# Memory attention in a hybrid encoder layer: its value products as three rounded passes over split operands, one fill place later

## Reference, cut to what matters

```python
proj = x @ w_in                       # r_q, r_k, ..., a_q, a_z are columns of it
mk, mv = jnp.split(mem @ xa_w_kv, 2, axis=-1)
s = jnp.einsum('blhd,bmhd->bhlm', q, mk).astype(jnp.float32) * XA_DH ** -0.5
p = jax.nn.softmax(s, -1)
xa = jnp.einsum('bhlm,bmhd->blhd', p, mv.astype(jnp.float32))
xa = xa * jax.nn.silu(a_z)
```

## Time and profile before

| | |
|---|---|
| Median of 3 runs | 1772.15 us (1770.97 to 1772.45) |
| The profiled execution | 1769.98 us, of which its span is 1767.8 us |
| PE busy | 1728.8 us, 98% of the span |
| PEld, DVE, ACT, POOL busy | 1438.5 (81%), 1034.6 (59%), 594.2 (34%), 538.2 (30%) us |
| Chain that ended last, by engine | PE 85%, DVE 7%, DMA 3%, ACT 2% |
| Granted TensorE clock | 0.998 of full speed over the span |

### The profile page before, as it was taken

The page is one execution under the profiler, slowest core; times in us unless marked ns, Lnnn a source line. Parts: engine busy times, 40 slices in busy tenths (PEclk is TensorE's granted clock), DMA queues, the critical chain, the costliest instruction groups (busy, mean ns, idle before and its releaser), DMA issues.

```text
span 1767.8 us, 22844 instructions
## 1 busy us (share of the span) xinstructions
PE 1728.8 (98%) x8848; PEld 1438.5 (81%) x8848; DVE 1034.6 (59%) x2022; ACT 594.2 (34%) x829; POOL 538.2 (30%) x342
## 2 busy tenths in 40 slices
PE   6989999999999999999999999999999999999998
PEld 5878888888787888888888788888878878888886
DVE  7889726562383477339847886253723825862625
ACT  5332334451125113432144332544311341143320
POOL 2543403022121313345355432121212141224451
PEclk9999999999999999999999999999999999999999
DMA  7435363242023206774433433541411222268441
GB/s 276 138 107 150 95 217 136 91 120 84 25 89 126 96 25 226 227 267 162 143 127 125 134 113 103 214 179 38 131 48 48 96 104 87 70 225 288 167 169 57
DMA packets 98707, 235.23 MB, mean 133 GB/s; under 512 B 10912, under 2 KB 41968, under 8 KB 97064
## 3 DMA queue, kind: packets, MB, share of 16 engines
q1 hardware_dynamic: 71688, 182.15, 30.5%
q10 hardware_dynamic: 26832, 51.39, 8.0%
q0 software_dynamic: 80, 0.23, 0.0%
HBM read 170.55 MB, written 58.98 MB: 130 GB/s over the span
## 4 chain that ended last, share of the span: by engine, by line
PE 85%; DVE 7%; DMA 3%; ACT 2%; issue 1%; POOL 1%; SPq 0%; ACTq 0%; DVEq 0%
PE gp L627 21%; PE gp L629 20%; PE gp L628 20%; PE mm L629 2%; PE mm L628 2%; PE mm L627 2%; DMA wraw<-in_w 2%; PE mm L855 2%; PE mm L833 2%; POOL wlo L1144 1%; PE mm L879 1%; PE mm L782 1%; DMA yraw<-yt 1%; PE mm L783 1%; PE mm L784 1%
## 5 line engine op out<-in xcount | busy, mean ns | idle before, releaser
L1144 POOL TENSOR_TENSOR wlo<-wraw,whi 128x256 fp32r<-128x256 f32 (+1 forms) x270 | 444.5, 1671 | 1026.2 <-ACT whi L1222 1026.0
L627 PE MATMUL gp<-xh,whi 128*128 128x512 f32 x768 | 319.0, 415 | 1.1 <-ACT xh L1292 1.1
L629 PE MATMUL gp<-xh,wlo 128*128 128x512 f32 x768 | 301.1, 392 | 0.0
L628 PE MATMUL gp<-xl,whi 128*128 128x512 f32 x768 | 299.8, 390 | 0.0
L627 PE MATMUL gp<-whi,xh 128*128 128x512 f32 x640 | 269.1, 420 | 0.0
L1222 ACT ACTIVATE whi<-wraw 128x1024 fp32r<-128x1024 f32 x164 | 168.4, 1054 | 263.5 <-DMA wraw<-in_w 108.6
L629 PE MATMUL gp<-whi,xl 128*128 128x512 f32 x640 | 250.5, 391 | 0.0
L628 PE MATMUL gp<-wlo,xh 128*128 128x512 f32 x640 | 249.9, 391 | 0.0
L629 PEld LDWEIGHTS gp<-xh,wlo 128*128 128x128 f32 x768 | 144.2, 188 | 32.0
L627 PEld LDWEIGHTS gp<-xh,whi 128*128 128x128 f32 x768 | 144.9, 189 | 29.7 <-issue 3.1
L628 PEld LDWEIGHTS gp<-xl,whi 128*128 128x128 f32 x768 | 144.9, 189 | 25.7
(11 more groups left out here) (335 smaller groups left out, 2928.4 us busy)
## 6 DMA issues: line engine op xcount, KB each, us to landing
wraw<-in_w SPq DMA_DIRECT2D x164, 512.0 KB, 4.1
spill<-gate ACTq DMA_DIRECT2D x32, 512.0 KB, 2.9
yraw<-yt SPq DMA_DIRECT2D x32, 512.0 KB, 5.8
xs<-xr SPq DMA_DIRECT2D x16, 512.0 KB, 5.4
xraw<-in_xT SPq DMA_DIRECT2D x4, 1024.0 KB, 16.0
ud<-gate ACTq DMA_DIRECT2D x8, 512.0 KB, 2.6
uu<-ud SPq DMA_DIRECT2D x64, 64.0 KB, 2.6
p_tab<-kd SPq DMA_DIRECT2D x64, 64.0 KB
```

The costliest lines, as they stand in the source:

```text
L627: nc.tensor.matmul(out, ah, bh, start=start, stop=False)
L628: nc.tensor.matmul(out, ah, bl, start=False, stop=False)
L629: return nc.tensor.matmul(out, al, bh, start=False, stop=stop)
L1144: last = nc.gpsimd.tensor_tensor(wlo[slot(u)][:, w0 + c:w0 + c + n], raw_view(l, u, i)[:, c:c + n], whi[slot(u)][:, w0 + c:w0 + c + n].bit ...
```

## The change

The values (mvT, once per layer) and each turned block of probabilities are split into a float32r high part and a remainder, and a value product becomes six passes of `mm3` in place of two fp32 products. ACT's copy out of bank[2] now writes the high part `pth`. DVE gets a new step per j, `x_low(j)`, which writes `ptl` = bank[2] - pth and then increments the new semaphore `x_pl`; it also gets `values_split`, a copy mvT to mvh and a subtraction to mvl (over mvT), which stands between `s5_product(3)` and `x_norm(0)` and is the first increment of `x_pl`. On DVE, `x_low` of step k stands at place XT[k], behind the `x_max` of that place, if it has one, and before its `x_norm`. PE's waits on `x_pt` become waits on `x_pl`: the turn j waits for `x_low(j-1)`, the value product j for `x_low(j)`. The value products move from XS + 5 to XS + 6 (the last one stays at 31), so `XV` becomes 8, 9, 11, 12, 14, 16, 17, 19, 20, 22, 24, 25, 27, 28, 30, 31. The load of mkT counts on the semaphore of the first two aq loads. DVE waits for the last value product before it writes `rot`, which lies where mvh and ptl are.

```diff
-XT, XV = [h + 3 for h in XS], [h + 5 for h in XS]
+XT, XV = [h + 3 for h in XS], [min(h + 6, 31) for h in XS]
...
-        pt = [at(f"pt{i}", 512, R[3] + 2048 + 512 * i) for i in range(2)]
+        mvh, mvl = at("mvh", 1024, R[2], F32R), at("mvl", 1024, R[3], F32R)
+        pth = [at(f"pth{i}", 512, R[3] + 2048 + 512 * i, F32R) for i in range(2)]
+        ptl = [at(f"ptl{i}", 512, R[2] + 1024 + 512 * i, F32R) for i in range(2)]
...
-                sp.dma_start(mkT, dram["kvs"][:, 0:1024]).then_inc(S["mk_in"], 16)
+                sp.dma_start(mkT, dram["kvs"][:, 0:1024]).then_inc(aq_in[0], 16)
...
                     if j == 0:
-                        pe.wait_ge(S["mk_in"], 16 * l + 16)
...
                     if j % 8 == 0:
-                        pe.wait_ge(aq_in[j // 8], 32 * l + 32)
+                        pe.wait_ge(aq_in[j // 8], (48, 32)[j // 8] * (l + 1))
...
                 def x_turn(j):
                     pe.wait_ge(S["x_norm"], XSTEPS * l + j + 1)
                     if j:
-                        pe.wait_ge(S["x_pt"], XSTEPS * l + j)
+                        pe.wait_ge(S["x_pl"], (XSTEPS + 1) * l + j + 1)
...
                 def x_values(j):
                     h = j // 4
-                    pe.wait_ge(S["x_pt"], XSTEPS * l + j + 1)
-                    if j == 0:
-                        pe.wait_ge(S["mv_in"], 16 * l + 16)
+                    pe.wait_ge(S["x_pl"], (XSTEPS + 1) * l + j + 2)
                     if j:
                         pe.wait_ge(S["x_pvev"], XSTEPS * l + j)
                     for m in range(2):
-                        last = nc.tensor.matmul(bank[3][:, 0:256], mvT[:, GW * m + 128 * h:GW * m + 128 * h + 128],
-                                                pt[j % 2][:, 256 * m:256 * m + 256], start=m == 0, stop=m == 1)
+                        v0 = GW * m + 128 * h
+                        last = mm3(bank[3][:, 0:256], mvh[:, v0:v0 + 128], mvl[:, v0:v0 + 128],
+                                   pth[j % 2][:, 256 * m:256 * m + 256], ptl[j % 2][:, 256 * m:256 * m + 256], m == 0, m == 1)
                     last.then_inc(S["x_pv"], 1)
...
-                pe.wait_ge(S["x_pt"], XSTEPS * l + XSTEPS)
+                pe.wait_ge(S["x_pl"], (XSTEPS + 1) * (l + 1))
...
-                    F(pt[j % 2], bank[2], ACT.Copy).then_inc(S["x_pt"], 1)
+                    F(pth[j % 2], bank[2], ACT.Copy).then_inc(S["x_pt"], 1)
...
+                def x_low(j):
+                    dve.wait_ge(S["x_pt"], XSTEPS * l + j + 1)
+                    TT(ptl[j % 2], bank[2], pth[j % 2].bitcast(F32), ALU.subtract).then_inc(S["x_pl"], 1)
+
+                def values_split():
+                    dve.wait_ge(S["mv_in"], 16 * l + 16)
+                    V.link(nc.vector.tensor_copy(mvh, mvT))
+                    TT(mvl, mvT, mvh.bitcast(F32), ALU.subtract).then_inc(S["x_pl"], 1)
...
                         x_max(j)
                         if j == 0:
                             s5_product(3)
+                            values_split()
+                        if hook in XT:
+                            x_low(XT.index(hook))
                         x_norm(j)
                         if l == 0 and j >= 6:
                             rope_angles(j - 6)
+                    elif hook in XT:
+                        x_low(XT.index(hook))
...
+                dve.wait_ge(S["x_pv"], XSTEPS * l + XSTEPS)
                 V.inc(TT(ra, a, co, ALU.mult))
```

More of the change, by code:

```diff
@@ L266, in build @@
             sp_out0 sp_out1 gate_in0 gate_in1 gate_used0 gate_used1 rt_done rt_free yt_out0 yt_out1 yt_out2 yt_out3
-            mt_done mt_free mk_in mv_in aq_in0 aq_in1 xo_out xo_in ring_in ring_used
-            x_s x_max x_e x_norm x_t x_pt x_pv x_pvev xa_out wif_in
+            mt_done mt_free mv_in aq_in0 aq_in1 xo_out xo_in ring_in ring_used
+            x_s x_max x_e x_norm x_t x_pt x_pl x_pv x_pvev xa_out wif_in
             wif_hi wif_lo if_done if_act if_sum rows_done rf_out ab_in wa_ev res_in colt_done cols_done wqk_in conv_done xc_ready
```

## The result

The changed kernel takes 1775.54 us in the median of 7 runs (1773.80 to 1778.59), the kernel before 1770.97 in the median of the 7 runs beside them. The ratio is 1.0029, 95% interval 1.0018 to 1.0040: slower by 5.1 us, 3.2 to 7.1 (the two medians alone differ by 4.6). Forecast were +4.9 us, slower, on a kernel before of 1772.15: 1777.0, with a range of 1770.5 to 1781.0.

What follows compares the result with a forecast made beforehand. PE's own list of work was taken to bound the attention stage. New waits of 9.2 us less 4.5 gained, plus about 0.2 for traffic, gave +4.9: 1777.0 us on the median, range 1770.5 to 1781.0.

Steps and rivals of the forecast that it cites:

- The gain: Value products on PE: six split passes take 0.72 us, saving 0.14 each, 32 times, 4.5 us.
- The third rival: Split product no cheaper than the old one, six passes at no less than 0.143 us each: 1781.6 us; chance 0.12.
- the estimate from the Trainium skill: Value product on PE at 2.4 GHz plus about 2.5 ns a pass: 0.66 us, gain 2 us larger in all.
- The start: Stage start: values_split before x_norm(0) delays DVE, so turn 1 waits for x_low(0), 1.5 us once per layer.
- The product copy's way round ACT: Moved products delay ACT's turn copy, exponentials and product copy, so the next product waits: 2.3 us per layer.
- the neighbour pairs: Products at 11/12 and 19/20 lose 0.68 us each; at 8/9, 16/17 and 24/25 0.32 each.
- Layer 0's own: Extra delays in layer 0 alone, from DVE's rope pieces, 1.1 us, and a held scaled maximum, about 0.5.
- The rope piece: Layer 0, scores at place 18: DVE's rope piece behind x_norm(10) delays exponentials(11) and product 8, 1.1 us more.
- The held step: Layer 0: step 12's scaled maximum, held 1.50 us in place of 0.17 while POOL worked, costs product 10 about 0.5.
- The 0.2 for added traffic: A guess: added DVE and ACT traffic beside PE's wide passes costs about 0.2 us.
- x_low for nothing: Each x_low takes 0.69 us of DVE, 16 per layer, at no cost where DVE waits for exponentials or is idle.
- What would show it: PE waits per layer: turn 1 about 1.5 us, three x_low waits some 0.2, five xo waits 0.1 to 0.7.

Runs made afterwards that it cites:

- the kernel that splits in the gap: Changed kernel with ACT copying mvT to mvh behind step 0's exponentials and DVE subtracting between x_max(1) and x_norm(1): median 1772.93 us, 1.0004 against the kernel before.

## Why the prediction was right, point by point

- **The gain.** 0.14 per product, 4.5 in all, was forecast; with the products at `h + 5` and the split in the gap the stages show 75.49 - 73.43 and 75.49 - 73.20, 4.35 together, and layer 1, where nothing is lost, 0.143 each. In the changed kernel the product takes 0.79 from 305.62 to the next wide pass where it follows a turn, the turn's 0.08 included. The third rival, no cheaper product, had 0.12 and fell. So did the smaller pass that the estimate from the Trainium skill had (TensorE: Matmul & The Clock Gate, "Wait — 56ns, not 53.3ns?"): the 0.12 of the earlier trace rows held between wide passes, and 0.66 per product would have given 2 us more than there was.
- **The start**, 1.5 per layer: 1.48 read, 1.51 and 1.48 by the kernel that splits in the gap. The copy of 128x1024, for which I had bounds of 0.69 and 1.226 and took the nearest form, is recorded as that very form, CAST, 0.69.
- **The product copy's way round ACT.** The mechanism stood; the term was too small. I let ACT see the product's end at V + 0.93, and the turn copy came at V + 1.05. 0.07 of the 0.12 is the product's first pass, longer behind a turn, as I had put in for PE and left out for ACT: the last pass starts at V + 0.67. The rest is the turn copy's own: it starts 0.38 after that pass in every row of layer 0 where it waits for a product, while a product copy with nothing ahead of it starts 0.32 after, the number that I took. The turn copy waits for two semaphores and the product copy for one; whether that is the reason no run tests. So the neighbour pairs lost 0.44 and 0.79 where 0.32 and 0.68 stood: 2.9 per layer in place of 2.3. That is the half microsecond missing in layer 1.
- **Layer 0's own.** The rope piece cost 1.04 at place 20 (1.68 idle against 0.64 in layer 1), 1.1 forecast. The held step, 0.5, did not cost: it was held for 0.77 in place of 1.50. Too much here and too little above cancel in layer 0, which is why that stage came out to 0.02. That is luck, and so in part is the total: the queue's term was 1.2 too small over both layers, the held step and the guess of 0.2 together 0.7 too large.
- **The 0.2 for added traffic**, a guess, was not borne out. Between two wide passes of one group lie 0.2303 us on the mean in layer 0's stage before and 0.2306 after, 0.2302 and 0.2305 in layer 1 (126 and 139 pairs in each). That would be 0.1 us in all, and the kernel with the move alone, without any of the added DVE work, has the same 0.2305.
- **x_low for nothing**: nearly. The kernels at `h + 5` have all of them and no wait but turn 1's, or none, in the waits view; start to start, layer 0 loses 0.13 and 0.09 to two of them.
- **What would show it**: four waits for x_low a layer, as said. For xo I said five times 0.1 to 0.7; the view has two a layer, since the three of 0.10 leave no idle row behind a turn that has just waited.

The parts do not simply add. The stages grow by 7.14 with the move alone and shrink by 1.29 with the split alone, together 5.85, and both are 5.32; in layer 1, 2.34 and 2.13. Why is open. The queue's own loss is nearly the same in both: in layer 1 of the move alone the pairs lose 0.37 three times and 0.80 twice, and five products behind a wait 0.08 each, 3.1 together; in the changed kernel it is 0.44 three times, 0.79 twice and 0.08 twice, also 3.1. So most of the 0.21 lies elsewhere, perhaps in what a product saves beside its new neighbours; no run took that apart.

## What to carry to other kernels

When a step is moved in the list of the engine that bounds the kernel, ask of every buffer it frees who waits for that, what stands behind the waiter in its queue, and whether the bounding engine wants one of those things back: here one place of delay for a step of 0.72 us on PE closed a loop PE, ACT, PE that cost 2.9 us per layer and that no busy share shows. New work on a half idle engine is free only in its idle stretches: 1.9 us in front of x_norm(0) cost 1.5 per layer, 1.2 in the gap behind x_max(1), with the copy on ACT, nothing. Moving work to an idle POOL is not moving it out of DVE's way.

## What I had not expected of the hardware

- A DVE step of 0.17 us, the scaled maximum, that meets a running POOL subtraction is let go only at that instruction's end: 1.50, 1.51 and 1.63 beside one of 1024 columns, 0.69 beside pieces of 256. In and around the two stages of the nine traces it met one 39 times. 35 times it was held, and ended within 0.03 of that end; the other four times under 0.2 us were left. Not every DVE step is held: the row maximum, which reads PSUM, started during such an instruction 40 times and always took its 0.69, and x_low, one of whose two inputs is in PSUM, 26 times, always 0.68 or 0.69.
- POOL waits in its turn. In the stages its 1024-column subtraction took 2.36 to 2.39 when no DVE step was in flight at its start, against 1.23 on DVE. Where x_norm or a rope piece, whose inputs are in SBUF, still had 0.26, 0.63 or 0.76 to run, it took 2.50, 2.87 and 3.00 to 3.02, and so ended 2.24 to 2.26 behind the end of that step each time. That is what makes its length vary here.
- PE idled up to 1.68 us at once, 4.7 in a stage of 78.7, and the granted clock stayed 1.00.
